# Two more places for part of an expert's weights, an earlier transfer, and fillers at the end of a stage

## The reference

```python
for e in range(N_EXPERTS):                                   # 32
    hid = jax.nn.silu(hf @ w_gate[e]) * (hf @ w_up[e])       # 1024 x 256 each
    y = y + (hid @ w_down[e]) * combine[:, e:e + 1]          # 256 x 1024
```

## Time and profile before

| what | value |
|---|---|
| median of three runs | 785.01 us |
| profiled execution: time, span | 784.17 us, 782.4 us |
| PE busy | 715.8 us (91%) |
| DVE, ACT busy | 324.4 us, 206.1 us |
| bytes moved by DMA, mean rate | 242.14 MB, 309 GB/s |
| matmuls of gate and up (L1540) | 125.9 us busy, 2016 records |

### The profile page before, as it was taken

The page is one execution under the profiler, slowest core; times in us unless marked ns, Lnnn a source line. Parts: engine busy times, 40 slices in busy tenths (PEclk is TensorE's granted clock), DMA queues, the critical chain, the costliest instruction groups (busy, mean ns, idle before and its releaser), DMA issues.

```text
span 782.4 us, 16674 instructions
## 1 busy us (share of the span) xinstructions
PE 715.8 (91%) x7436; PEld 458.6 (59%) x7436; DVE 324.4 (41%) x688; ACT 206.1 (26%) x414; POOL 31.6 (4%) x99
## 2 busy tenths in 40 slices
PE   9999999999989998999899999999998975787696
PEld 7778787658646564565447746785764542343342
DVE  7476976535353422333136064542445321221222
ACT  2575577215100000000042354530520000000003
POOL 7006000000000000000000000000000000000000
PEclk9999999999999997999999999999999998988999
DMA  8644113499999999999999822009999999999995
GB/s 265 199 102 147 55 57 111 154 424 377 355 420 421 420 421 421 420 420 421 412 345 371 260 85 78 1 15 420 416 394 422 420 421 418 421 421 421 420 406 201
DMA packets 72069, 242.14 MB, mean 309 GB/s; under 512 B 9846, under 2 KB 37612, under 8 KB 51260
## 3 DMA queue, kind: packets, MB, share of 16 engines
q1 hardware_dynamic: 71788, 240.52, 78.6%
q10 hardware_dynamic: 208, 0.54, 0.2%
HBM read 240.00 MB, written 1.05 MB: 308 GB/s over the span
## 4 chain that ended last, share of the span: by engine, by line
PE 65%; DMA 19%; DVE 6%; SPq 4%; ACT 3%; issue 2%; PEld 0%; POOL 0%; PEldq 0%; ACTq 0%; POOLq 0%
DMA M<-in_m_w_down_dram 12%; PE ps L1857 10%; PE ps L1540 9%; PE ps L1077 8%; DMA M<-in_m_w_gate_dram 7%; PE ps L1384 7%; PE ps L1485 5%; PE ps L1612 4%; PE ps L1500 4%; SPq L448 2%; SPq L442 2%; DVE H L2471 1%; PE ps L1023 1%; PE ps L1399 1%; PE ps L1751 1%
## 5 line engine op out<-in xcount | busy, mean ns | idle before, releaser
L1540 PE MATMUL ps<-M 128*32 128x256 f32 x2016 | 125.9, 401 | 23.5 <-DMA M<-in_m_w_gate_dram 16.9
L1540 PEld LDWEIGHTS ps<-M 128*32 128x32 f32 x2016 | 67.1, 115 | 80.6 <-DMA M<-in_m_w_gate_dram 18.6
L1077 PE MATMUL ps<-M 128*128 128x272 f32 x352 | 85.7, 398 | 0.0
L1857 PE MATMUL ps<-M 128*128 128x256 f32 (+2 forms) x288 | 79.9, 434 | 0.0
L1485 PEld LDWEIGHTS ps<-M 128*128 128x128 f32 x608 | 71.5, 192 | 12.2 <-issue 11.7
L1485 PE MATMUL ps<-M 128*128 128x128 f32 x608 | 76.9, 278 | 0.0
L1077 PEld LDWEIGHTS ps<-M 128*128 128x128 f32 x352 | 65.9, 191 | 15.4 <-issue 1.7
L1612 PE MATMUL ps<-M 128*32 128x512 f32 x448 | 56.5, 649 | 15.3 <-DMA M<-in_m_w_down_dram 15.3
L1500 PE MATMUL ps<-M 128*128 128x512 f32 (+1 forms) x120 | 62.8, 647 | 5.4 <-DVE H L2471 5.4
L1857 PEld LDWEIGHTS ps<-M 128*128 128x128 f32 x288 | 53.7, 190 | 22.6 <-issue 15.6
L2468 DVE TENSOR_TENSOR H<-H,ps 128x512 f32<-128x512 f32 x60 | 41.3, 688 | 59.7 <-PE ps L1500 59.5
(11 more groups left out here) (462 smaller groups left out, 839.5 us busy)
## 6 DMA issues: line engine op xcount, KB each, us to landing
M<-in_m_w_gate_dram SPq DMA_DIRECT2D x31, 2048.0 KB, 19.4
M<-in_m_w_down_dram SPq DMA_DIRECT2D x26, 2048.0 KB, 22.7
M<-in_m_w_up_dram SPq DMA_DIRECT2D x25, 2048.0 KB, 22.6
M<-in_o_w_in_dram SPq DMA_DIRECT2D x12, 1024.0 KB, 9.6
M<-in_e_w_in_dram SPq DMA_DIRECT2D x11, 1024.0 KB, 5.8
M<-in_m_w_down_dram SPq DMA_DIRECT2D x9, 1024.0 KB, 18.7
M<-in_m_w_up_dram SPq DMA_DIRECT2D x8, 1024.0 KB, 20.9
M<-in_e_w_out_dram SPq DMA_DIRECT2D x4, 1024.0 KB, 5.1
```

The lines of the kernel that those rows point to most:

```text
L1077: ins = pe.matmul(ps[:, n % 4, 0:T], wringE[:, (n // 2) % 4, k, (n % 2) * P:(n % 2) * P + P], (xnE if n else xuE)[:, k], start=(k == 0), s ...
L1540: ins = pe.matmul(ps[32 * e:32 * e + 32, 3 * x, 0:FF], xgT[q % 2][:, k, 32 * e:32 * e + 32], w, start=(k == 0), stop=(k == KD - 1))
L1857: ins = pe.matmul(ps[rows, unit % 4, 0:n], lhs(k), rhs(k), start=(k == 0), stop=(k == KD - 1))
```

## The change

In the first expert stage unit 1 is cut differently. Slot 2 takes expert 0 whole and the second halves of experts 1 to 3. The first halves of experts 1, 2 and 3 go to `apart[1]` = `xgT[1]`, `apart[2]` = columns 33792 to 34815 of M (where `sil`, `hid` and `hidT` lie later) and `apart[3]` = `yst[0]`, and the up products over k < 4 read them there. The one for expert 1 can't be issued before the router is through with `hrT`, which covers `xgT[1]` (`lg_done` 2, signalled by the last router products); it is now the last piece of unit 1. So the places of three first halves in slot 2 are free earlier, and the first halves of `down[5:8]` (1536 KB) are issued behind `res_done` 5, ahead of the last pieces of unit 1; `down[4]`'s (512 KB) is left behind `half_done` 2. ACT's first `sil` also waits for `half_done` 2. Layer 0 gets the two fillers before `last_down`.

```diff
--- before.py
+++ after.py
@@ -286,6 +286,7 @@
         level, cmp = at(31616, NE, 8), at(31616 + 8 * NE, 16, NE)
 
         aside = [[K0[:, 0:D], K1[:, 0:D], yst[1]], [K0[:, 0:D], K1[:, 0:D], at(26624, D), yst[1]]]
+        apart = [None, xgT[1].rearrange("p k t -> p (k t)"), at(33792, D), yst[0]]
         fnb = H[:, 2, :]
         fin = at(D, 2, D)
         ROOT_BANK = [1, 5]
@@ -361,11 +362,12 @@
                     for e in (0, 2):
                         sp.dma_start(slots[j][:, e:e + 2, :], src[:, e:e + 2, :]).then_inc(s(f"ld_s{j}"), 16)
 
-                def but_quarter(u, src, rest):
+                def but_quarters(u, src, rest):
                     j = UNIT_SLOT[y][u]
-                    sp.dma_start(slots[j][:, 0:2, :], src[:, 0:2, :]).then_inc(s(f"ld_s{j}"), 16)
-                    sp.dma_start(slots[j][:, 2, :], src[:, 2, :]).then_inc(s(f"ld_s{j}"), 16)
+                    sp.dma_start(slots[j][:, 0, :], src[:, 0, :]).then_inc(s(f"ld_s{j}"), 16)
+                    sp.dma_start(slots[j][:, 1:3, D:2 * D], src[:, 1:3, D:2 * D]).then_inc(s(f"ld_s{j}"), 16)
                     sp.dma_start(slots[j][:, 3, D:2 * D], src[:, 3, D:2 * D]).then_inc(s(rest), 16)
+                    sp.dma_start(apart[2], src[:, 2, 0:D]).then_inc(s(rest), 16)
 
                 if y == 0:
                     sp.wait_ge(s("sa_evac"), NC)
@@ -379,7 +381,7 @@
                         continue
                     if y == 0 and u == 1:
                         sp.wait_ge(s("mixE"), NC)
-                        but_quarter(u, up[:, 0:4], "ld_pv_ys")
+                        but_quarters(u, up[:, 0:4], "ld_pv_ys")
                         for e in range(2):
                             set_aside(e)
                         continue
@@ -399,9 +401,13 @@
                         if y == 0:
                             sp.wait_ge(s("res_done"), 5)
                             sp.dma_start(slots[j][:, 2, :], gate[:, 6, :]).then_inc(s("ld_wout"), 16)
+                            sp.dma_start(slots[UNIT_SLOT[y][5]][:, 1:4, 0:D], down[:, 5:8, 0:D]).then_inc(s("ld_lruw_e5"), 16)
                             sp.wait_ge(s("res_done"), 6)
-                            sp.dma_start(yst[0], up[:, 3, 0:D]).then_inc(s("ld_pv_ys"), 16)
+                            sp.dma_start(apart[3], up[:, 3, 0:D]).then_inc(s("ld_pv_ys"), 16)
                             sp.dma_start(slots[j][:, 3, :], gate[:, 7, :]).then_inc(s(f"ld_s{j}"), 16)
+                            set_aside(2)
+                            sp.wait_ge(s("lg_done"), 2)
+                            sp.dma_start(apart[1], up[:, 1, 0:D]).then_inc(s("ld_pv_ys"), 16)
                             continue
                         sp.wait_ge(s("res_done"), 11)
                     elif u == OV_NEXT:
@@ -410,15 +416,14 @@
                         else:
                             sp.wait_ge(s("ov_fin"), y + 1)
                     elif u == 4:
-                        set_aside(2 + y)
-                        if y == 0:
-                            sp.dma_start(slots[UNIT_SLOT[y][5]][:, 3, 0:D], down[:, 7, 0:D]).then_inc(s("ld_lruw_e5"), 16)
+                        if y == 1:
+                            set_aside(3)
                         if y == 0:
                             sp.wait_ge(s("half_done"), 1)
                             sp.dma_start(slots[j][:, 3, 0:D], up[:, 7, 0:D]).then_inc(s("ld_half"), 16)
                             sp.dma_start(slots[j][:, 0:3, 0:D], up[:, 4:7, D:2 * D]).then_inc(s(f"ld_s{j}"), 16)
                             sp.wait_ge(s("half_done"), 2)
-                            sp.dma_start(slots[UNIT_SLOT[y][5]][:, 0:3, 0:D], down[:, 4:7, 0:D]).then_inc(s(f"ld_s{UNIT_SLOT[y][5]}"), 16)
+                            sp.dma_start(slots[UNIT_SLOT[y][5]][:, 0, 0:D], down[:, 4, 0:D]).then_inc(s(f"ld_s{UNIT_SLOT[y][5]}"), 16)
                             wait_through(UNIT_PREV[y][u])
                             sp.dma_start(slots[j][:, 3, D:2 * D], up[:, 7, D:2 * D]).then_inc(s(f"ld_s{j}"), 16)
                             continue
@@ -816,6 +821,8 @@
                 for q in range(NQ):
                     n = NQ * y + q
                     act.wait_ge(s("gate_done"), n + 1)
+                    if n == 0:
+                        act.wait_ge(s("half_done"), 2)
                     nc.scalar.activation(sil, ps[:, 0, 0:FF], ACT.Silu).then_inc(s("sil"), 1)
                     act.wait_ge(s("rt_done"), n + 1)
                     nc.scalar.activation(RT[q % 2], ps[:, 6, 0:T], ACT.Copy).then_inc(s("rt_set"), 1)
@@ -1517,7 +1524,7 @@
                     j = UNIT_SLOT[y][u]
                     pe.wait_ge(s(f"ld_s{j}"), 32 * (FIRST_LAYER[j] * y + UNIT_TURN[y][u] + 1))
                     if y == 0 and u == 1:
-                        pe.wait_ge(s("ld_pv_ys"), 272)
+                        pe.wait_ge(s("ld_pv_ys"), 304)
                     elif y == 0 and u == 3:
                         pe.wait_ge(s("ld_wout"), 80)
                     elif y == 0 and u == 5:
@@ -1535,8 +1542,8 @@
                                 w = aside[y][e][:, FF * k:FF * k + FF]
                             elif u == 4 and k >= KD // 2 and (e < 3 or y == 1):
                                 w = gu_w[UNIT_SLOT[y][u]][:, e, k - KD // 2, :]
-                            elif u == 1 and y == 0 and k < KD // 2 and e == 3:
-                                w = yst[0][:, FF * k:FF * k + FF]
+                            elif u == 1 and y == 0 and k < KD // 2 and e:
+                                w = apart[e][:, FF * k:FF * k + FF]
                             ins = pe.matmul(ps[32 * e:32 * e + 32, 3 * x, 0:FF], xgT[q % 2][:, k, 32 * e:32 * e + 32], w,
                                             start=(k == 0), stop=(k == KD - 1))
                         if u < 2 and k == KD // 2 - 1:
@@ -1688,8 +1695,7 @@
                                             start=True, stop=True)
                     ins.then_inc(s("cb"), 1)
 
-                if y == 1:
-                    keep_busy(2, 4)
+                keep_busy(2, 4)
                 pe.wait_ge(s("ld_last0"), 32 * (y + 1))
                 last_down(0, 512, 4).then_inc(s("dn_done"), 1)
                 pe.wait_ge(s("rt_set"), n + 1)
```

## The result

The changed kernel takes 789.12 us (median of 22 runs, 784.31 to 790.76) against 785.21 us (22 runs, 782.81 to 787.4). The ratio is 1.0042, 95% interval 1.003 to 1.0054: slower by 3.3 us (2.4 to 4.2). This ratio is not the quotient of the two medians, which lie 3.9 us apart. The forecast was 2.5 us more, a median of 787.5 in a range of 783.8 to 790.2.

What follows compares the result with a forecast made beforehand. The prediction took the first expert stage to be bound by its DMA bytes. A queue term of 1.2 us plus 1.3 us for fillers made 2.5 us, from 785.01 to 787.5 us, range 783.8 to 790.2.

Steps and rivals of the forecast that it cites:

- Unit 1's landing: First expert stage: unit 1's last piece lands at 199.0 us, so PE, wanting it at 196.03, waits 3.0 us.
- Counting the bytes ahead of the piece from the last known landing: Unit 1's landing: gate quarter landing at 189.6, then 4 MB taking 10.0 us, giving 199.6.
- the sum from the rates: Unit 1's landing: the aside's earlier landing at 196.4, less 1.8 us regained, plus 3.75 us for 1536 KB, giving 198.35.
- The clock behind the wait: First group on PE: products behind the wait run at a lower clock, costing 1.2 us (0 to 1.7).
- PE's lateness is what costs: First group: wait and clock make PE's signals 4.2 us late, so group 2 is issued at 214.7 instead of 210.54.
- The queue's term: Before group 2: the queue empties and the stage's transfer stream comes 1.2 us later, at most 2.8.
- With 3.0 the final 2 MB land: Queue before group 2: with a 3.0 us restart, 2 MB issued at 207.4 land at 215.4; group 2 moves at 217.7.
- The fillers' term: End of layer 0's expert stage: two fillers delay the last down products by 1.3 us (0 to 1.3).
- there is no slow stretch to cure: End of layer 0: last down block takes 1.92 us without fillers, so fillers have no slow clock to mend.
- the case in which they are hidden: End of layer 0: fillers cost 0 if PE gets there 1.3 us earlier against the landings, as without the slow clock.
- The gain rival: First expert stage: pauses close, PE doesn't wait, 4.8 us return less 1.3 for fillers, 781.5 us; chance 0.13.
- the 4.8 us of lost time: Start of the first expert stage: DMA time lost against 420 GB/s before the queue stays full.

Runs made afterwards that it cites:

- e1: The changed kernel without its two new fillers in layer 0; 788.4 against 784.57 us for the kernel before, ratio 1.0046.
- e3: The changed kernel, fillers kept, with unit 1's last piece issued ahead of the gate quarter and the aside; 782.91 us, ratio 0.9979 to the kernel before.
- e4: The changed kernel without fillers, with unit 1's last piece issued ahead of the gate quarter and the aside; 783.12 us, ratio 0.9986 to the kernel before.
- e7: The kernel before with three products of ones on PE between the wait for unit 1 and its first products; 786.16 us, ratio 1.0025.
- e8: The kernel before with five products of ones on PE between the wait for unit 1 and its first products; 786.82 for 784.11 us, ratio 1.0039.
- e2: The kernel before with only the two layer 0 fillers added; 784.94 for 784.57 us, ratio 1.0007.
- e5: The changed kernel without fillers, the early 1536 KB of down sent behind unit 1's last piece; 784.03 for 784.11 us of the kernel before, ratio 0.9994.
- e6: The changed kernel without fillers, 512 KB of early down left in place, 1024 KB behind unit 1's last piece; 785.12 for 784.11 us of the kernel before, ratio 1.0007.
- e10: The kernel of e3, fillers kept, with only 512 KB of down ahead of unit 1's last pieces; 783.76 against 784.68 us for the kernel before, ratio 0.9988.
- e9: The same program as e3, run once more; 783.86 against 784.68 us for the kernel before, ratio 0.9991.

## Why the prediction was right, and where it wasn't

**Unit 1's landing: right, at the late end.** Forecast 199.0 (198.35 to 199.6), which is 19.95 us (19.3 to 20.55) behind the issue of the third gate quarter. PE went on at 199.38, 20.62 us behind it, and at 198.67 in e1, 20.55 us behind it. The wait was 3.48 us in e1 and 2.01 in the profile of the changed kernel, where PE had come late by the slow clock at 190. Counting the bytes ahead of the piece from the last known landing gave 199.6 and was right to 0.1 us; the sum from the rates gave 198.35 and was 1.2 us early.

**The clock behind the wait: right.** 1.2 us forecast (0 to 1.7); 1.6 in the profile (3.40 and 1.78 for 1.93 and 1.60) and 1.6 in e1.

**PE's lateness is what costs: right, and shown.** Group 2 was forecast at 214.7, 4.2 us late, and issued at 215.63 (214.74 in e1). Counted from the third gate quarter it was 5.4 us late, and 5.1 in e1, where the wait (3.48) and the clock (1.6) account for it. Taking the wait away (e3, e4) takes the whole loss away; adding lateness to the old kernel (e7, e8) costs 2.0 us for 2.84 of lateness and 3.1 for 4.56. Together with e1's 3.6 for 5.1, each microsecond of lateness costs about 0.7.

**The queue's term: too small.** I had 1.2 us (up to 2.8); e1, which has no fillers, shows 3.6 us in time (1.9 to 5.3), and the lost DMA time rose by 8.4 - 4.8 = 3.6 us. The step that failed was "With 3.0 the final 2 MB land at 207.4 + 3.0 + 5.0 = 215.4, and the queue is empty when group 2's transfers start to move at 214.7 + 3.0 = 217.7". They were issued 0.9 us later than that, at 208.28, and landed at 218.3; group 2's first transfer landed at 225.4, 4.0 us later than the 210.54 + 10.9 = 221.4 of before. I had costed two pauses with full rate between them. The runs show a queue that is never quite empty behind 208 but slow: SP's pieces come singly, behind PE's signals at 202.82, 206.56 and 208.28, the rate falls to 82 GB/s from 206 to 208, averages 279 from 208 to 218, and is back at 421 in the stretch from 222 on. Why it stays low while 2.5 MB are queued is not shown.

**The fillers' term: too large.** 1.3 us forecast (0 to 1.3), about 0 found: e2 is 0.5 us slower than the kernel before, the change 0.3 us faster than e1, e3 0.5 us faster than e4, all by their ratios. Each pair has an uncertainty of over 1 us, and e2's interval alone would allow 1.3; the three together speak against it. The fillers stand in the profile as forecast, but the step "there is no slow stretch to cure" took one execution for all, although the same paragraph named the case in which they are hidden. Where the last gate block is slow (the changed kernel, e2), PE comes late and fillers delay it. Where it isn't, PE idles 2.5 us before the last down products (e1, e4, e5, e7). Without fillers these then take 3.2 to 3.4 us for 1.92 in three profiles (e1, e4, e5) and 1.93 in one (e7). That the two cases about cancel fits the medians; it was not tested by itself. So the sum came out near the measured one by luck in its parts, with two errors of opposite sign: by the central values a queue term short by 2.4 us and a filler term long by 1.3.

**The gain rival** rested on unit 1 being in time. e3 puts that condition right, and then only 0.1 to 0.2% comes of the 4.8 us of lost time. The queue's losses move and hardly shrink: each of e3, e4, e5 and e6 still loses about 4.3 us from 186 to 222 by its stretches, as the old program does in e2's profile, at 196 to 202 in e3 and at 202 to 216 in e5. Only e10 loses less, 3.2 us, without a time to show for it beyond e9's. A likely reason is that until 196 us only so many places are free, and when they are filled the queue must wait for PE's signals whatever the order; that was argued from the stretches, not tried. Whether e3 is really a little faster, and why, stays open.

## What to carry to other kernels

Where all transfers share one queue, sending a piece early delays every piece behind it: add up the bytes ahead of the one that an engine waits for next, and put that one first. A wait of an in-order engine that also frees the places has to be priced with the queue: its signals come late, and the queue runs dry meanwhile. Here PE's lateness came through to the end at about 0.7 of its length, though PE had idle time later in the stage. Judge a filler over several executions, since one profile shows only one of the clock's courses.

## What the runs showed of the hardware that I had not expected

The granted clock can fall in one execution and not in another at the same instructions. PE was busy for 5.2 us of the 6 from 186 to 192 both in the changed kernel's profile, where the clock was 0.50 at 190 to 192, and in e1's, where it was 1.00 throughout. The gathers near 188 us took 2.92 us in six of the twelve profiled executions (the kernel before, e1, e2, e5, e8, e10) and 4.54 us in the other six (the changed kernel, e3, e4, e6, e7, e9); e1 has the changed kernel's program up to there, and e7 the old one. So the slow stretch at 190 us doesn't need the change; whether the change makes it more frequent (five of eight profiles of its kind, one of four of the old) can't be told from so few. It isn't the loss: e3, e4 and e9 have it and lose nothing. The same holds for the last gate block of layer 0, 3.66 us in e1, 5.35 in e2 and 6.41 in e6, each behind 3.3 to 3.4 us of idle.
